# Gate and up projections of a mixture-of-experts stage as three fp32r products

## The chip, the cores and the metric

One core of a Trainium2 chip runs the whole program. The metric is device time in microseconds: the median of three runs of the kernel before is 1720.55 us (1717.99 to 1735.88). TensorE (PE in the views) does the matrix products and transposes, VectorE (DVE) and ScalarE (ACT) the elementwise work, GpSimd (POOL) and SyncE (SP) issue most of the DMAs.

## The reference

Two decoder layers over 1024 rows of width 1024. Each has a token mixer and then a mixture of experts in which every row goes to 2 of 16 experts of inner width 256:

```python
x = x + jnp.concatenate([att, pool], axis=-1) @ w_out[l]
h = rms_norm(x, norm2_gain[l])
# router: one of 4 groups, then two of its 4 experts, gates = softmax weights
hg = jnp.einsum('td,edf->tef', t, w_gate)
hu = jnp.einsum('td,edf->tef', t, w_up)
a = jax.nn.silu(hg) * hu * gates[..., None]
y = jnp.einsum('tef,efd->td', a, w_down)
x = x + y
```

The token mixer is h @ w_in (four groups of 512 columns), an attention of 8 heads over a dilated mask, and a pooling group. All is float32.

## The kernel before

Each engine runs a program of its own, written by hand; semaphores join them. One loop over the two layers holds five stages: input projection, attention, pooling and output projection with the router's logits, routing, experts.

In the input and output projections each factor is already split into a high part (a copy rounded to fp32r) and a low part (the float32 value minus it), and three fp32r products (high x high, high x low, low x high) are added in PSUM. ScalarE makes the high part of the weights (in_high, L661), VectorE the low part (in_low, L938).

**Experts.** The (row, expert) pairs are sorted into blocks of 128 rows of one expert: at most 31 (BLOCKS), of which the first `used` count. The first 16 are unconditional (`SURE`), each later one is under a comparison with `used`. In the order of each engine, for block t:
- GpSimd gathers the rows of a block from DRAM with an indirect DMA (load_rows, L608) as soon as a slot of a ring of three is free, and adds the result of a block five earlier to the output with another (add_rows, L618).
- TensorE (moe_pe, L1591): gate_up(t), one float32 product per 128 of K, so 8 of 128x512 into PSUM bank 2, 16 passes in the trace (L1566), on weights that stay where the DMA put them; xtm(t+1), eight transposes of the next block's rows (L1340); down(t-1), four products 128x512 (L1579); two transposes of the activation of t.
- ScalarE (moe_act, L841): Silu (L843); half of the y copy of t-1 (moe_down, L834), then a wait for y0_ready, y1_ready and the landed additions (s_add); then aT (L847), the transposed activation that down(t) reads.
- VectorE (moe_dve, L1281): rows_evac(t+1), the transposed rows times norm2's gain in two instructions of 128x512 (L905); the activation product (L1285); y_evac(t-1), its half of y (L1270).

The weights of an expert (gate, up and down, 1 MB each) lie in one of four slots. SyncE issues the load of expert e+4 when the down product of expert e's last block is done, and reports expert e+3 after that (report, w_loaded):

```python
sp.wait_ge(dn_done, upto(l, BLOCKS, ended))                      # L516
load_expert(e, slot)
report((slot - 1) % SLOTS, g if i else g - 1)
```

TensorE reads the expert of a block from the table block_e into a register, waits for w_loaded, and works out the address (weights, L1557). After the last block, the rest of the 31 are passed through the conditional's other branch on every engine, and the next layer's first rows are read back (L461), squared (L657) and normalised.

**Around it.** While routing runs, SyncE loads the first 512 columns of the next layer's w_in (L504), ScalarE and VectorE split them (L828, L1279). The gate of each listed row comes out of 16 small products (L1586) that stand before gate_up(0). In the attention VectorE evacuates part of the transposed probabilities (half_evac, L1057) and adds the mask and takes the maximum of the scores two row blocks ahead (mask, L1040), in that order. In the output projection it normalises each row tile (L1134) and scales its transposed columns by the gain (gain2, L1108).

## Time and profile before

| | |
|---|---|
| median of three runs | 1720.55 us |
| profiled execution, its own time | 1728.34 us |
| its span, first to last instruction | 1726.4 us |
| TensorE busy | 1493.9 us (87%) |
| VectorE, ScalarE, GpSimd busy | 782.2, 453.9, 315.3 us |
| gate and up products, L1566 (720 passes) | 325.8 us |
| down products, L1579 (360 passes) | 165.2 us |
| chain that ended last | PE 76%, DVE 8%, issue 7%, DMA 3% |
| DMA | 221.09 MB, mean 128 GB/s |

The profiled execution is one run with the hardware profiler on. Busy times are unions of an engine's records; records of TensorE overlap, so the pitch between starts, not the length of a record, is what one product costs. "Issue" is time in which an engine waited for nothing that the profile shows. The expert stage of layer 0 runs from about 558 to 826 us, that of layer 1 from about 1404 to 1684 us.

### The profile page before, as it was taken

What the parts mean: (1) busy time and instruction counts of PE and PEld (TensorE: products, weight loads), DVE (VectorE), ACT (ScalarE), POOL (GpSimd) and SP (SyncE); (2) the same over time, 40 slices, a digit from 0 to 9 for tenths busy, and PEclk for the clock granted to TensorE, in tenths of its full rate; (3) what the DMA queues carried; (4) which work ended last, traced back from release to release, by engine and by line L of the source; (5) the groups of instructions that cost most, each with busy time, mean ns of one, the idle gap of its engine ahead of it and who ended that gap; (6) DMA issues with size and microseconds to landing.
All of it is one profiled execution on the core that took longest, in us unless ns stands there. A gap on an engine that the chain in (4) does not pass through costs nothing.

```text
span 1726.4 us, 22556 instructions
## 1 busy us (share of the span) xinstructions
PE 1493.9 (87%) x6963; PEld 1080.2 (63%) x6964; DVE 782.2 (45%) x1883; ACT 453.9 (26%) x886; POOL 315.3 (18%) x204
## 2 busy tenths in 40 slices
PE   5999978998993999999389998889899759999990
PEld 4878868886882444444178786788788624444440
DVE  5777656663337122212267866666534452212210
ACT  4231245762111011111222313557412101111110
POOL 1000067001000122222500002930200012222224
PEclk9999989999995999999599999999999869999995
DMA  8000020000168599973960002000002945999947
GB/s 313 18 1 0 0 98 1 2 1 1 73 225 286 163 286 297 339 216 85 233 214 0 1 0 98 1 1 2 1 26 96 332 143 161 272 297 287 307 86 159
DMA packets 116624, 221.09 MB, mean 128 GB/s; under 512 B 5976, under 2 KB 72736, under 8 KB 116544
## 3 DMA queue, kind: packets, MB, share of 16 engines
q1 hardware_dynamic: 91744, 131.82, 22.1%
q0 software_dynamic: 19136, 69.38, 16.5%
q10 hardware_dynamic: 5664, 18.88, 2.8%
q8 instruction: 44, 0.72, 0.2%
q14 instruction: 36, 0.29, 0.1%
HBM read 170.77 MB, written 49.28 MB: 127 GB/s over the span
## 4 chain that ended last, share of the span: by engine, by line
PE 76%; DVE 8%; issue 7%; DMA 3%; ACT 2%; POOL 1%; ACTq 1%; DVEq 0%; PEld 0%; PEldq 0%; POOLq 0%; SPq 0%
PE ps L1566 19%; PE ps L1360 17%; PE ps L1340 10%; PE ps L1493 10%; PE ps L1579 9%; PE ps L1446 6%; PE ps L1420 2%; PE ps L1507 2%; DMA out_x<-x_res,arena 2%; PE ps L1422 1%; POOL out_x L622 1%; DVE k_high L1031 1%; DVE arena L1149 1%; PE ps L1480 1%; DVE w_in_lo L944 1%
## 5 line engine op out<-in xcount | busy, mean ns | idle before, releaser
L1566 PE MATMUL ps<-big,arena 128*128 x720 | 325.8, 606 | 9.7 <-issue 8.3
L1340 PE MATMUL ps<-cst,arena 128*128 128x128 f32 x1242 | 186.8, 286 | 78.2 <-DVE arena L915 36.4
L1566 PEld LDWEIGHTS ps<-big,arena 128*128 128x128 f32 x720 | 135.8, 194 | 170.5 <-issue 170.5
L905 DVE TENSOR_TENSOR arena<-ps,par 128x512 f32<-128x512 f32 x126 | 81.1, 686 | 355.6 <-PE ps L1340 355.6
L1340 PEld LDWEIGHTS ps<-cst,arena 128*128 128x128 f32 x1242 | 153.0, 147 | 125.3 <-DVE arena L915 38.1
L1360 PE MATMUL ps<-w_in_hi,hT_hi 128*128 128x512 f32 x512 | 206.1, 403 | 13.2 <-DVE hT_lo L933 10.5
L1360 PE MATMUL ps<-w_in_lo,hT_hi 128*128 128x512 f32 x512 | 202.1, 395 | 0.0
L1360 PE MATMUL ps<-w_in_hi,hT_lo 128*128 128x512 f32 x512 | 201.9, 394 | 0.0
L614 POOL DMA_INDIRECT x_res<-token_rows,row_tok x62 | 61.0, 984 | 607.0 <-issue 310.3
L1579 PE MATMUL ps<-big,arena 128*128 x360 | 165.2, 602 | 5.4 <-issue 5.4
L1446 PE MATMUL ps<-big,arena 128*128 128x64 f32 x1152 | 148.5, 276 | 0.0
L1446 PEld LDWEIGHTS ps<-big,arena 128*128 128x128 f32 x1152 | 145.2, 199 | 1.3
L622 POOL DMA_INDIRECT out_x<-x_res,arena x62 | 102.8, 1658 | 170.3 <-ACTq L839 141.1
L1052 DVE CUSTOM_DVE_ANT_0 arena<-ps,cst 128x128 f32<-128x128 f32 (+7 forms) x128 | 96.3, 752 | 56.0 <-PE ps L1422 55.5
L754 ACT ACTIVATE arena<-arena,st 128x128 f32<-128x128 f32 (+7 forms) x128 | 98.9, 772 | 82.5 <-DVE st L1052 82.0
L1360 PEld LDWEIGHTS ps<-w_in_hi,hT_hi 128*128 128x128 f32 x512 | 97.8, 191 | 35.5 <-issue 12.0
L1579 PEld LDWEIGHTS ps<-big,arena 128*128 128x128 f32 x360 | 66.0, 194 | 72.4 <-issue 72.4
L1360 PEld LDWEIGHTS ps<-w_in_hi,hT_lo 128*128 128x128 f32 x512 | 97.8, 191 | 21.2
L1493 PE MATMUL ps<-w_o_hi,cat_hi 128*128 128x512 f32 x256 | 104.1, 407 | 7.2 <-DVE cat_lo L1115 7.2
L1360 PEld LDWEIGHTS ps<-w_in_lo,hT_hi 128*128 128x128 f32 x512 | 98.0, 191 | 19.4
L1493 PE MATMUL ps<-w_o_lo,cat_hi 128*128 128x512 f32 x256 | 101.5, 396 | 0.0
L1493 PE MATMUL ps<-w_o_hi,cat_lo 128*128 128x512 f32 x256 | 101.3, 396 | 0.0
(169 smaller groups left out, 1771.3 us busy)
## 6 DMA issues: line engine op xcount, KB each, us to landing
big<-in_w_gate SPq DMA_DIRECT2D x32, 1024.0 KB, 7.9
big<-in_w_up SPq DMA_DIRECT2D x32, 1024.0 KB, 12.7
big<-in_w_down SPq DMA_DIRECT2D x32, 1024.0 KB, 15.4
big<-in_w_in SPq DMA_DIRECT2D x16, 1024.0 KB, 9.9
big<-in_w_out SPq DMA_DIRECT2D x4, 2048.0 KB, 10.2
token_rows<-arena ACTq DMA_DIRECT2D x16, 512.0 KB, 3.2
out_x<-x_res ACTq DMA_DIRECT2D x16, 512.0 KB, 3.9
x_res<-out_x SPq DMA_DIRECT2D x8, 512.0 KB, 6.0
```

What stands on the lines that cost most here:

```text
L614: pool.indirect_dma_start(out=xg[slot], out_offset=None, in_=token_rows, in_offset=bass.IndirectOffsetOnAxis(ap=row_tok[:, j:j + 1], axis= ...
L622: pool.indirect_dma_start(out=out, out_offset=bass.IndirectOffsetOnAxis(ap=row_dst[:, j:j + 1], axis=0), in_=y[j % RING], in_offset=None, ...
L754: sc.activation(pr[m % 3][:, 0:nk], pr[m % 3][:, 0:nk], ACT.Exp, scale=-1.0, bias=st[:, 64 + m % 16:65 + m % 16], accum_out=st[:, 80 + m % ...
L905: ins = ve.tensor_tensor(out=dst[:, 4 * h:4 * h + 4, :], in0=ps[:, banks + h, :].rearrange("p (a c) -> p a c", c=P), in1=spread(gain[:, 4 ...
L1052: ve.tensor_tensor_reduce(out=pr[m % 3][:, 0:nk], in0=ps[:, 2 * b:2 * b + 2, :].rearrange("p a c -> p (a c)")[:, 0:nk], in1=cst[:, C_MASK ...
L1340: ins = te.transpose(ps[:, bank + i // 4, (i % 4) * P:(i % 4 + 1) * P], src, ident)
L1360: ins = te.matmul(ps[:, 2 + 2 * par_ + i, :], a[par_][:, k, :], b[:, k, :], start=k == 0 and n == 0, stop=k == K - 1 and n == 2)
L1420: te.matmul(ps[:, 2 * b + c // 512, 0:w], q_parts[a][:, i * P:(i + 1) * P], k_high[a][:, c:c + w], start=True, stop=False)
L1446: ins = te.matmul(ps[:, 6 + hd % 2, i * HD:(i + 1) * HD], prT[b][:, j, :], v[:, j, hd * HD:(hd + 1) * HD], start=j == 0, stop=j == i)
L1493: ins = te.matmul(ps[:, 2 * par_ + h, :], a[par_][:, k, :], b[:, k, :], start=k == 0 and n == 0, stop=k == K - 1 and n == 2)
L1566: ins = te.matmul(ps[:, 2, :], xgT[:, k, :], big[:, ds(at + k * 2 * FE, 2 * FE)], start=k == 0, stop=k == K - 1)
L1579: ins = te.matmul(ps[:, 4 + h, :], aT[:, k, :], big[:, ds(at + (E_GU + k * D + 512 * h), 512)], start=k == 0, stop=k == 1)
```

## The change

The gate and up product becomes 24 fp32r products of 128x512. The weights of a block are split in halves of 128x2048 (K 0 to 3 and 4 to 7): gu_high on ScalarE, gu_low on VectorE, into a ring of three halves, high and low each. They are split again for every block, also where it has the same expert as the one before. A half is overwritten when the product of the half three before is done (gu_half). The rows are split too: rows_high on ScalarE, rows_evac on VectorE, one instruction of 128x1024 each, into xgT_hi and xgT_lo. Both gu_high and gu_low read the block's expert from block_e into a register each time. The gain of norm2 is multiplied into the rows before they are stored (gain2_row, a broadcast load), not after the transposes. The first input weights of the next layer are loaded when expert 12 has ended, and split after the last block. list_gates moves behind gate_up(0), and mask before half_evac.

```diff
-        xgT = A[:, 3072:4096].rearrange("p (k n) -> p k n", n=P)
-        sg, act = A[:, 4096:4352], A[:, 4352:4608]
+        xgT_hi = nc.alloc_sbuf_tensor_at("xgT_hi", [P, D], f32r, offset=xr_start)[:, :].rearrange("p (k n) -> p k n", n=P)
+        xgT_lo = nc.alloc_sbuf_tensor_at("xgT_lo", [P, D], f32r, offset=xr_start + 4 * D)[:, :].rearrange("p (k n) -> p k n", n=P)
+        HALF_GU = K * 2 * FE // 2
+        gu_hi = [part(f"gu_hi{i}", at, HALF_GU) for i, at in enumerate((0, 2 * HALF_GU, AT_A))]
+        gu_lo = [part(f"gu_lo{i}", at + HALF_GU, HALF_GU) for i, at in enumerate((0, 2 * HALF_GU, AT_A))]
+        gain2_row = A[:, 0:D]
+        experts = big[:, :]
+        sg, act = A[:, 7904:8160], A[:, 4352:4608]
...
@@ -475,6 +488,7 @@
                 sp.wait_ge(rows_t, 1)
                 sp.wait_ge(x_ready, upto(l, T, T))
                 load_in(l, 2, 1)
+                sp.wait_ge(win_split, upto(l, 8, 2))
...
+                sp.dma_start(gain2_row, norm2_gain[ds(l, 1), :].to_broadcast([P, D])).then_inc(s_gain2, 16)
...
-                load_in((l + 1) % DEPTH, 0, 0)
...
                 report(1, NE // SLOTS - 1)
+                with sp.If(l < DEPTH - 1):
+                    ended = sp.value_load(start_i[0:1, NE - 3:NE - 2], min_val=0, max_val=BLOCKS)
+                    sp.wait_ge(dn_done, upto(l, BLOCKS, ended))
+                    load_in((l + 1) % DEPTH, 0, 0)
...
-                in_high(l + 1, 0)
...
+                def gu_high(t, slot, h):
+                    e = a_.value_load(block_e[0:1, ds(t, 1)], min_val=0, max_val=NE - 1)
+                    a_.wait_ge(w_loaded, upto(l, NE, e + 1))
+                    a_.sem_inc(s_passed, 1)
+                    at = ((e + 2) % SLOTS) * E_ALL + AT_E
+                    sc.activation(gu_hi[(2 * slot + h) % 3], experts[:, ds(at + h * HALF_GU, HALF_GU)],
+                                  ACT.Copy).then_inc(gu_top, 1)
+                def rows_high(t):
+                    a_.wait_ge(xtm_done, upto(l, BLOCKS, t + 1))
+                    sc.activation(xgT_hi, ps[:, 0:2, :].rearrange("p a (k n) -> p (a k) n", n=P), ACT.Copy)\
+                        .then_inc(xg_top, 1)
...
                 def moe_act(t, slot, m):
+                    if not last(t, BLOCKS):
+                        gu_high(t + 1, (slot + 1) % RING, 0)
+                        a_.wait_ge(gu_half, upto(l, BLOCKS, t + 1))
+                        a_.sem_inc(s_passed, 1)
+                        gu_high(t + 1, (slot + 1) % RING, 1)
                     a_.wait_ge(gu_done, upto(l, BLOCKS, t + 1))
                     sc.activation(sg, ps[:, 2, 0:FE], ACT.Silu).then_inc(silu_done, 1)
+                    if not last(t, BLOCKS):
+                        a_.wait_ge(xgT_ready, upto(l, BLOCKS, t + 1))
+                        rows_high(t + 1)
                     if not first(t):
                         moe_down(t - 1, *before(slot, m))
...
+                for h in range(2):
+                    gu_high(0, 0, h)
+                for i in range(2):
+                    a_.wait_ge(s_tok[i], (l + 1) * (16 * (T // 2)) + 1)
+                    a_.sem_inc(s_passed, 1)
+                a_.wait_ge(s_base, (l + 1) * (16 * T))
+                a_.sem_inc(s_passed, 1)
+                rows_high(0)
...
                     ch.restart()
+                    in_high(l + 1, 0)
...
@@ -1077,10 +1131,10 @@
                 mask(1)
                 for m in range(ROWS_A):
                     p, n = m // 16, m % 16
+                    if m + 2 < ROWS_A:
+                        mask(m + 2)
                     if m % T >= 4:
                         half_evac(m)
-                    if m + 2 < ROWS_A:
-                        mask(m + 2)
                     if m >= T and m % T == 1:
...
-                    times_gain(h2T[par_], par[:, G2:G2 + K], 4, h2T_ready)
+                    ve.tensor_copy(h2T[par_], ps[:, 4:6, :].rearrange("p a (k n) -> p (a k) n", n=P)).then_inc(h2T_ready, 1)
...
-                    ve.tensor_scalar(xs2[par_], xr[:, t, :], r, None, ALU.mult).then_inc(xs2_ready, 1)
+                    ve.scalar_tensor_tensor(out=xs2[par_], in0=xr[:, t, :], scalar=r, in1=gain2_row,
+                                            op0=ALU.mult, op1=ALU.mult).then_inc(xs2_ready, 1)
...
+                def gu_low(t, slot, h):
+                    dve.wait_ge(gu_top, upto(l, 2 * BLOCKS, 2 * t + h + 1))
+                    dve.sem_inc(s_passed, 1)
+                    e = dve.value_load(block_e[0:1, ds(t, 1)], min_val=0, max_val=NE - 1)
+                    at = ((e + 2) % SLOTS) * E_ALL + AT_E
+                    i = (2 * slot + h) % 3
+                    ve.tensor_tensor(out=gu_lo[i], in0=experts[:, ds(at + h * HALF_GU, HALF_GU)],
+                                     in1=gu_hi[i].bitcast(f32), op=ALU.subtract).then_inc(gu_split, 1)
+                for h in range(2):
+                    gu_low(0, 0, h)
...
                 def rows_evac(t):
-                    dve.wait_ge(xtm_done, upto(l, BLOCKS, t + 1))
-                    times_gain(xgT, par[:, G2:G2 + K], 0, xgT_ready)
+                    dve.wait_ge(xg_top, upto(l, BLOCKS, t + 1))
+                    ve.tensor_tensor(out=xgT_lo, in0=ps[:, 0:2, :].rearrange("p a (k n) -> p (a k) n", n=P),
+                                     in1=xgT_hi.bitcast(f32), op=ALU.subtract).then_inc(xgT_ready, 1)
...
-                in_low(l + 1, 0)
                 def moe_dve(t, slot, m):
                     if not last(t, BLOCKS):
-                        rows_evac(t + 1)
+                        for h in range(2):
+                            gu_low(t + 1, (slot + 1) % RING, h)
                     dve.wait_ge(silu_done, upto(l, BLOCKS, t + 1))
                     ve.scalar_tensor_tensor(out=act, in0=ps[:, 2, FE:2 * FE], scalar=list_gate[:, ds(t, 1)], in1=sg,
                                             op0=ALU.mult, op1=ALU.mult).then_inc(a_ready, 1)
+                    if not last(t, BLOCKS):
+                        rows_evac(t + 1)
                     if not first(t):
                         y_evac(t - 1, *before(slot, m))
...
                 with dve.If(l < DEPTH - 1):
+                    in_low(l + 1, 0)
...
-                def gate_up(t):
-                    at = weights(t)
+                def gate_up(t, slot):
                     for k in range(K):
-                        ins = te.matmul(ps[:, 2, :], xgT[:, k, :], big[:, ds(at + k * 2 * FE, 2 * FE)],
-                                        start=k == 0, stop=k == K - 1)
+                        h = k // (K // 2)
+                        if k % (K // 2) == 0:
+                            pe.wait_ge(gu_split, upto(l, 2 * BLOCKS, 2 * t + h + 1))
+                        c = slice(k % (K // 2) * 2 * FE, (k % (K // 2) + 1) * 2 * FE)
+                        hi, lo = gu_hi[(2 * slot + h) % 3][:, c], gu_lo[(2 * slot + h) % 3][:, c]
+                        for n, (a, b) in enumerate(((xgT_hi, hi), (xgT_hi, lo), (xgT_lo, hi))):
+                            ins = te.matmul(ps[:, 2, :], a[:, k, :], b, start=k == 0 and n == 0,
+                                            stop=k == K - 1 and n == 2)
+                        if k == K // 2 - 1:
+                            ins.then_inc(gu_half, 1)
                     ins.then_inc(gu_done, 1)
...
                 xtm(0, 0, 0)
-                pe.wait_ge(gate_parts, upto(l, 1, 1))
-                for c in range(2 * T):
-                    ins = te.matmul(ps[:, 7, 0:96], in_row[:, c, :], in_gate[:, c, :, :].rearrange("p k b -> p (k b)"),
-                                    start=c == 0, stop=c == 2 * T - 1)
-                ins.then_inc(gates_listed, 1)
                 used = pe.value_load(start_i[0:1, NE:NE + 1], min_val=2 * SEQ // P, max_val=BLOCKS)
+                def list_gates():
+                    pe.wait_ge(gate_parts, upto(l, 1, 1))
+                    for c in range(2 * T):
+                        ins = te.matmul(ps[:, 7, 0:96], in_row[:, c, :],
+                                        in_gate[:, c, :, :].rearrange("p k b -> p (k b)"),
+                                        start=c == 0, stop=c == 2 * T - 1)
+                    ins.then_inc(gates_listed, 1)
                 def moe_pe(t, slot, m):
                     pe.wait_ge(xgT_ready, upto(l, BLOCKS, t + 1))
                     if not first(t):
                         pe.wait_ge(a_ready, upto(l, BLOCKS, t))
                     pe.sem_inc(s_passed, 1)
-                    gate_up(t)
+                    gate_up(t, slot)
+                    if first(t):
+                        list_gates()
```

Line numbers in the order listings below are those of each version; L1339 of after is y_evac, L886 is aT, L865 the half of y on ScalarE, L859 rows_high, L1333 rows_evac, L1354 the activation product.

ScalarE, body of the loop over blocks, before:

```order
L843 ACTIVATE arena<-ps 128x256
L832 ISA
L833 ISA
L834 ACTIVATE x_res<-ps 128x512
L838 ISA
L847 ACTIVATE arena<-ps 128x256
```

and after, up to the register read of the next turn:

```order
L854 ACTIVATE gu_hi_75<-big 128x2048
L879 ACTIVATE arena<-ps 128x256
L858 ISA
L859 ACTIVATE xgT_hi<-ps 128x1024
L863 ISA
L864 ISA
L865 ACTIVATE x_res<-ps 128x512
L869 ISA
L886 ACTIVATE arena<-ps 128x256
L850 ISA
L850 TENSOR_LOAD block_e
L850 ISA x2
```

The copy of aT (L847, now L886) is followed by a register read (TENSOR_LOAD) and the first high half of the block after the next, where only the next wait for TensorE stood.

VectorE, body of the same loop, before:

```order
L1264 ISA
L905 TENSOR_TENSOR arena<-ps,par 128x512 x2
L1285 ISA
L1285 SCALAR_TENSOR_TENSOR arena<-ps,arena 128x256
L1269 ISA
L1270 COPY x_res<-ps 128x512
```

and after, from the register read of the second half on:

```order
L1303 TENSOR_LOAD block_e
L1303 ISA x2
L1306 ISA
L1306 TENSOR_TENSOR gu_lo_78<-big,gu_hi_75 128x2048
L1353 ISA
L1354 ISA
L1354 SCALAR_TENSOR_TENSOR arena<-ps,arena 128x256
L1332 ISA
L1333 TENSOR_TENSOR xgT_lo<-ps,xgT_hi 128x1024
L1337 ISA
L1338 ISA
L1339 COPY x_res<-ps 128x512
```

The rows' evacuation moved behind the activation product, and two subtractions with a register read each stand before it.

VectorE at the start of the expert stage, before (block_e is the table of experts, gate_w the gates whose bits are taken apart):

```order
L1238 TENSOR_SCALAR block_e<-arena 128x32
L1243 ISA
L1246 TENSOR_SCALAR arena<-gate_w 128x16
L1247 TENSOR_SCALAR arena<-gate_w 128x16
L1248 TENSOR_SCALAR arena<-gate_w 128x16
L1249 CAST arena<-arena 128x48
```

and after:

```order
L1294 TENSOR_SCALAR block_e<-arena 128x32
L1301 ISA
L1303 TENSOR_LOAD block_e
L1303 ISA x2
L1306 ISA
L1306 TENSOR_TENSOR gu_lo_76<-big,gu_hi_73 128x2048
L1301 REGISTER_ALU
L1303 TENSOR_LOAD block_e
L1303 ISA x2
L1306 ISA
L1306 TENSOR_TENSOR gu_lo_77<-big,gu_hi_74 128x2048
L1311 ISA
```

Both subtractions of block 0 now stand between the table of experts and the gate bits.

## Rows read from the trace of the kernel before

**Rows 1.** The chain of waits, one block: start us, us, what
```profile
619.40 6.87 PE ps L1566 x16
...
627.14 3.44 PE ps L1579 x8
630.58 0.22 PE ps L1340 x2
```

**Rows 2.** Windows: length, busy us per engine (instructions), clock, DMA share
```profile
280.00:390.00 110.00, 104.06 (x807) 96.66 (x806) 68.05 (x145) 74.08 (x156) 14.71 (x5) 0.99 0.01 1
570.00:820.00 250.00, 244.08 (x716) 117.61 (x714) 49.79 (x84) 29.02 (x64) 53.00 (x42) 0.99 0.80 239
640.00:650.00 10.00, 9.93 (x31) 4.73 (x30) 0.94 (x2) 1.36 (x3) 2.00 (x2) 1.00 1.06 358
```

**Rows 3.** TensorE timeline, input projection: start us, us, engine line operation
```profile
108.66 0.39 PE L1360 MATMUL ps<-w_in_hi,hT_lo 128*128 128x512 f32 x1
108.88 0.39 PE L1360 MATMUL ps<-w_in_hi,hT_hi 128*128 128x512 f32 x1
```

**Rows 4.** Timeline, the operations that price a split of weights and rows
```profile
532.82 3.69 ACT L667 ACTIVATE w_in_hi<-big 128x2048 fp32r<-128x2048 f32 x2
...
514.87 1.22 DVE L1127 TENSOR_TENSOR x_res<-ps,x_res 128x1024 f32<-128x1024 f32 x1 [4.17 <-PE ps L1493]
...
558.15 4.49 DVE L944 TENSOR_TENSOR w_in_lo<-big,w_in_hi 128x2048 fp32r<-128x2048 f32 x2
```

**Rows 5.** Timeline of ScalarE and VectorE in the expert stage, one block
```profile
650.30 1.29 DVE L905 TENSOR_TENSOR arena<-ps,par 128x512 f32<-128x512 f32 x2 [7.60 <-PE ps L1340]
651.51 0.47 DVE L1285 SCALAR_TENSOR_TENSOR arena<-ps,arena 128x256 f32<-128x256 f32 x1
653.89 0.69 DVE L1270 COPY x_res<-ps 128x512 f32<-128x512 f32 x1 [1.91 <-PE ps L1579]
...
654.83 0.39 ACT L847 ACTIVATE arena<-ps 128x256 f32<-128x256 f32 x1 [0.37 <-DVE x_res L1270]
```

**Rows 6.** First product; register reads, ns min/median/max, first and last start
```profile
558.53 8.58 PE L1566 MATMUL ps<-big,arena 128*128 x16 [1.25 <-issue]
...
L1559 PEldq TENSOR_LOAD <-block_e x5: 298/303/310, 641.3 to 663.8; - x5
...
L1260 DVEq TENSOR_LOAD <-start_i x2: 326/438/550, 554.4 to 1399.7; - x2
```

**Rows 7.** Timeline, start of the expert stage: routing known, gate bits, second product
```profile
549.96 0.18 DVE L1238 TENSOR_SCALAR block_e<-arena 128x32 int32<-128x32 f32 x1
...
554.12 0.19 DVE L1258 SCALAR_TENSOR_TENSOR arena<-ps,arena 128x32 int32<-128x32 f32 x1
...
571.45 8.83 PE L1566 MATMUL ps<-big,arena 128*128 x16 [1.25 <-issue]
```

**Rows 8.** Timeline of SyncE's queue: two loads of expert weights, first and last transfer
```profile
1568.88 0.37 SPq L486 DMA_DIRECT2D big<-in_w_gate  x1
...
1570.08 1.95 SPq L489 DMA_DIRECT2D big<-in_w_down  x1
...
1603.68 0.37 SPq L486 DMA_DIRECT2D big<-in_w_gate  x1
...
1606.37 5.46 SPq L489 DMA_DIRECT2D big<-in_w_down  x1
```

**Rows 9.** Timeline of ScalarE at the end of layer 0
```profile
846.45 1.28 ACT L877 ACT_TABLE_LOAD   x1 [20.12 <-ACTq L857]
```

**Rows 10.** Timeline of VectorE in the attention
```profile
353.92 0.56 DVE L1062 COPY arena<-ps 128x384 f32<-128x384 f32 x1 [1.32 <-PE ps L1340]
```

**Rows 11.** Timeline of GpSimd and VectorE, start of layer 1
```profile
854.94 1.55 POOL L622 DMA_INDIRECT out_x<-x_res,arena  x1 [0.30 <-issue]
856.80 5.89 POOL L622 DMA_INDIRECT out_x<-x_res,arena  x1 [0.31 <-issue]
...
856.78 4.48 DVE L944 TENSOR_TENSOR w_in_lo<-big,w_in_hi 128x2048 fp32r<-128x2048 f32 x2
```

24 lines of the change are left out of this document (20 added, 4 removed).

## The prediction

> **What bounds the kernel now.** I read the page first: TensorE is busy 87% of the span and holds 76% of the chain that ended last, so the chain, followed through the expert stage, comes next. There every block of 128 rows is the same four pieces on TensorE with nothing between them: 16 passes of the gate and up product in 6.87 us, eight transposes in the 0.87 up to 627.14, the down product 3.44, two transposes 0.22 [rows 1]. That is 11.40 us a block, and the windows show TensorE busy 244 of 250 us there, with VectorE at 20% and ScalarE at 12% [rows 2]. The count of the passes (720 = 45 x 16) gives 45 blocks, 22 in layer 0 and 23 in layer 1. The DMA engines are the second resource: while every block has an expert of its own they stand at a share of 1.06 and 358 GB/s [rows 2]. So TensorE is the bound, the transfers are close behind it, and ScalarE and VectorE have some 9 us a block to spare. That spare time is what the change spends.
>
> **The product itself.** A 128x512 fp32r product is recorded at 0.39 us, but the records overlap: in the input projection they start every 0.227 us [rows 3]. Gate and up become 24 of them: 24 x 0.227 = 5.45 us in place of 6.87. If TensorE stayed the bound a block would take 5.45 + 0.87 + 3.44 + 0.22 = 9.98 us, 1.42 less, or 64 us over 45 blocks. That is the ceiling, not the forecast.
>
> **The loop that the change closes.** Each block's weights must now be split: two 128x2048 copies on ScalarE (3.69 for two, 1.85 each) and two 128x2048 subtractions on VectorE (4.49 for two, 2.24 each) [rows 4]. Look at the order around them. On VectorE a turn of the loop is: first subtraction, second subtraction, the activation product, the rows' low part, and only then the copy of y from PSUM. On ScalarE the copy of aT waits for that y copy (its wait for y0_ready), and the next block's first high half stands behind aT; VectorE's next first subtraction waits for that half. So the loop runs through both engines and holds one block:
> - activation product to rows' low part, 0.40 (a 0.47 record, 0.08 overlapped, as all pitches on VectorE);
> - rows' low part, 128x1024 with one input in PSUM. Nearest row: 1.22 for the same shape in the output projection [rows 4]; pitch 1.14. Floor: the two 128x512 evacuations, of which the second ends 1.29 after the start and the next starts at 1.21 [rows 5];
> - y copy 0.69, and from its end to the start of aT 0.25 (653.89 + 0.69 to 654.83) [rows 5];
> - aT's start to the first high half: a register read of the block's expert lies between. On TensorE the same read with its wait and addresses leaves 1.25 us idle when nothing covers it [rows 6]; on ScalarE 0.38 of it runs under aT's own 0.38. I take 1.0;
> - the high half, 1.85;
> - its end to the first subtraction: a register read on VectorE, bare. The read proper is 0.14 longer there than on TensorE (0.44 and 0.30), and no register has to be waited for [rows 6]; I take 1.1;
> - first subtraction 2.24, second 2.20. The second one's register read is taken as hidden under the first, because TensorE reads block_e while its own matmuls still run (five reads in a stretch without a gap, 0.30 each) [rows 6].
>
> Sum: 0.40 + 1.14 + 0.69 + 0.25 + 1.0 + 1.85 + 1.1 + 2.24 + 2.20 = 10.87 us. That is longer than TensorE's 9.98, so TensorE idles 0.9 us a block and the block costs 10.87, only 0.53 less than now. Bounds: register reads that cost 0.3 each give 9.5, and then TensorE's 9.98 holds; a second read that is not hidden gives 11.9. With 41 blocks behind the first two of each layer: -0.53 x 41 = **-22 us**, bounds -58 and +20.
>
> **The start of each expert stage.** The first two splits stand on VectorE before the gate bits. Routing is known at 550.14 [rows 7]. Two register reads on ScalarE, 0.9 each, put the first high half at 552.0 to 553.9, VectorE's two subtractions at 555.0 to 559.5, the gate bits (3.8 us, now ending at 554.31 [rows 7]) behind them to 563.3, a register read to 564.2, the rows' low part to 565.4. The product starts at 565.5 where it started at 558.53 [rows 6]: 7 us late. Then the list of gates, moved behind it on TensorE, and the second block's subtractions, which stand behind its evacuation, hold the first activation product: 565.5 + 7.5 (at part clock, as the 8.58 and 8.83 us of the first two blocks now) + 0.75 + 0.8 + 0.9 + 4.5 + 1.6 = 581.8, against 571.45 [rows 7]. The second block's shorter product returns about 1. **+9.4 us** a layer, 19 in all; bounds 6 and 13 a layer.
>
> **Expert loads.** Four slots hold weights, and load e+4 is issued when expert e ends. The report that expert e+3 is in comes only after that load is queued. Queueing takes 3.1 us on a quiet queue (1568.88 to 1572.03) and 8.2 behind an unfinished load (1603.68 to 1611.83) [rows 8]. Now the report is wanted at the start of block b+3, b being e's last block, when the two experts between have one block each; after the change ScalarE wants it a block earlier, at its high half, some 3.0 us after the down product that frees the slot. Ten first blocks stand so (five in each layer, by the issue times); these two are the shortest and the longest queueing among them, which is 0.1 to 5.2 too much, some 22 us in all. A wait lets the transfers catch up, so neighbours do not add; a shorter block makes them lag more (a load with a block's rows takes some 12.1 us at 358 GB/s: 4.2 MB). I take 7 a layer, **+14 us**, bounds 4 and 30.
>
> **The rest.** At the layer's end ScalarE comes to its table load at 846.45 straight from its own queue [rows 9], and TensorE waits for what follows. The split of the first input weights, which lay in the routing stage, now stands before it: two copies, 3.7 us, **+4**, once. In the attention the mask two row blocks ahead no longer stands behind the evacuation of the second half, which waits for transposes (1.32 us in [rows 10]). TensorE idles 5.9 of 110 us there [rows 2], so at most 7 a layer come back; I take **-3** for both, bounds 0 and -10. Folding norm2's gain makes the normalised rows a two-tensor operation (about 1.2 for 0.75), on the path for the last tile alone: **+1**. The 2 MB load and its split that leave the routing stage cost nothing now: VectorE did that split (558.15 to 562.64) under the first product [rows 4]. The broadcast of the gain (0.5 MB) has a projection of 11 us to land under.
>
> Sum: -22 + 19 + 14 + 4 - 3 + 1 = +13 us on the profiled execution's 1728.3 us, which is 0.5% above the median of 1720.55: **1734 us** as a median.
>
> **A rule against the change.** The two indirect DMAs of each block are generated on GpSimd, an addition in 1.55 us. One took 5.89: it started at 856.80, with two VectorE subtractions of SBUF tensors from 856.78 to 861.26 [rows 11]. After the change every block has such a pair. The Trainium skill (SBUF — State Buffer, Who interferes with whom) says that a VectorE operation with two SBUF inputs takes only the read side from GpSimd, and infers that descriptor generation goes on beside it. By that rule the sum stays; by the row each block's gather or addition can come 4.3 us late. The measurement decides. A gather has two blocks of slack, and an addition starts at 1.7 us of a block, ahead of the subtractions at 4.9, so my sum holds no term for it.
>
> **The rivals.**
> - *Register reads are cheap (0.30).* For: one VectorE read took only 0.33, and queues can run ahead. Against: 1.25 us stood bare on TensorE [rows 6]. The loop is then 9.5 to 10.3 and TensorE holds near 10.1: -1.3 x 41 = -53, but the waits for loads grow (+22): -53 + 19 + 22 + 2 for the rest = -10, 1711 us; with the start and the attention at their kind bounds (-6, -7), 1698.
> - *VectorE's second read is bare (0.18), the other side.* For: every read in VectorE's rows stands behind a wait, none under a running operation. A read that waits for the engine to drain adds 1.0 to the loop: 11.9 us. It decides from 11.4 us a block: above that the blocks lose. +0.5 x 41 = +20, hardly a wait for loads (+1): 20 + 19 + 1 + 2 = +42, 1762 us.
> - *Transfers or additions are the bound (0.15).* Runs of one-block experts go at 12.1 us, each with a queueing wait, or the additions of [rows 11] come late: 12 us more than forecast, some 1748. For: shares of 1.06. Against: pauses of several blocks in the loads.
> - *Forecast (0.37)*: 1722 to 1748.
>
> **How the numbers follow.** About 1% is what a measurement here can tell from no change: 1703 to 1738. Faster by over 1%: somewhat over half of the first rival (1698 to 1722, with its middle at 1711; the loop's terms leave more room below than above), 0.18. Slower by over 1%: nearly all of the second rival (0.16), most of the third (0.11) and three tenths of the forecast's case (0.11): 0.38. Within: 0.44. Range: from the cheap reads with the kind start, 1700, to the bare read, 1762.
>
> **What would show it.** Product starts 0.227 apart at 24 a block; a block of 10.9 us with 0.9 idle on TensorE, released by VectorE's low part; VectorE near 80% busy; the first product near 565; high halves that wait for a load where two one-block experts precede; PE restart at the layer's end 4 us later against the last down product. Blocks of 10.1 or 11.9 would break the loop's terms, and a start within 3 us of now the second term.

## The result, and the profile after

The changed kernel's median is 1784.05 us (four runs, 1772.11 to 1789.20) against 1728.22 for the kernel before in the same session: a recorded ratio of 1.028, 95% interval 1.023 to 1.034 (the two medians alone give 1.032). It is slower, by more than the 1% that can be told, and above the predicted range (1700 to 1762). In all ratios, runs more than 1.5% above the fastest run of the same kernel are left out. Its profiled execution took 1789.2 us, span 1787.3: 61 us more than the span before, and the longest of its four runs. Parts that vary from run to run are therefore also read from the experiments below.

From the page of the changed kernel, busy times, chain, and groups (line, engine, operation, count, busy us, mean ns, idle before and its releaser):

```profile
PE 1454.7 (81%) x7323; PEld 1154.7 (65%) x7324; DVE 987.4 (55%) x1913; ACT 669.6 (37%) x1026; POOL 363.6 (20%) x204
...
PE 53%; DVE 14%; issue 12%; ACT 8%; DVEq 3%; DMA 3%; ACTq 3%; SPq 2%; POOL 1%; PEld 0%; PEldq 0%; POOLq 0%
...
L1306 DVE TENSOR_TENSOR gu_lo<-big,gu_hi 128x2048 fp32r<-128x2048 f32 x94 | 212.9, 2291 | 255.6 <-issue 227.8
...
L854 ACT ACTIVATE gu_hi<-big 128x2048 fp32r x94 | 179.2, 1915 | 152.4 <-issue 127.3
L632 POOL DMA_INDIRECT x_res<-token_rows,row_tok x62 | 111.3, 1795 | 598.6 <-issue 310.2
...
L1644 PE MATMUL ps<-gu_hi,xgT_hi 128*128 128x512 f32 x360 | 153.0, 425 | 61.3 <-DVE xgT_lo L1333 61.3
```

TensorE is busy 39 us less, and holds 53% of the chain instead of 76%. VectorE, ScalarE, their queues and "issue" hold 40%. Before the subtractions stand 255.6 idle us, 227.8 of them ended by the engine's own issue. The window of the expert stage, one of those of [rows 2], in the changed kernel (span, us, busy time and count of TensorE, its weight loads, VectorE, ScalarE and GpSimd, granted clock, DMA share, GB/s):

```profile
570.00:820.00 250.00, 213.80 (x867) 146.28 (x866) 133.96 (x103) 124.44 (x122) 73.05 (x39) 0.96 0.81 242
```

TensorE, 244 of 250 us busy before, is now busy 214. Its granted clock in this window is 0.96 where it was 0.99. One unstalled block of layer 0, timeline of VectorE and ScalarE (start, length, both in us, idle before in brackets):

```profile
604.05 0.48 DVE L1354 SCALAR_TENSOR_TENSOR arena<-ps,arena 128x256 f32<-128x256 f32 x1
...
605.57 0.68 DVE L1339 COPY x_res<-ps 128x512 f32<-128x512 f32 x1
...
606.48 0.38 ACT L886 ACTIVATE arena<-ps 128x256 f32<-128x256 f32 x1 [0.79 <-DVE x_res L1339]
...
607.50 1.92 ACT L854 ACTIVATE gu_hi<-big 128x2048 fp32r x1 [0.64 <-issue]
...
610.07 1.92 ACT L854 ACTIVATE gu_hi<-big 128x2048 fp32r x1 [0.65 <-issue]
...
610.57 4.68 DVE L1306 TENSOR_TENSOR gu_lo<-big,gu_hi 128x2048 fp32r<-128x2048 f32 x2 [4.31 <-issue]
...
615.16 0.48 DVE L1354 SCALAR_TENSOR_TENSOR arena<-ps,arena 128x256 f32<-128x256 f32 x1
```

Activation products at 604.05 and 615.16: the block takes 11.11 us, where it took 11.40. The next one, at whose start the hardware loop turns (every third block):

```profile
619.28 3.94 ACT L854 ACTIVATE gu_hi<-big 128x2048 fp32r x2 [1.01 <-issue]
...
623.29 4.49 DVE L1306 TENSOR_TENSOR gu_lo<-big,gu_hi 128x2048 fp32r<-128x2048 f32 x2 [5.92 <-ACT gu_hi L854]
...
627.70 0.48 DVE L1354 SCALAR_TENSOR_TENSOR arena<-ps,arena 128x256 f32<-128x256 f32 x1
```

12.54 us. The first high half ends at 621.21 and the first subtraction starts at 623.29, 2.1 us later, where 1.1 lay in the block before (609.42 to 610.57). The chain of waits names the piece, a register read of VectorE, and below it stands what the same line takes in all (min, median and max in ns):

```profile
619.28 1.93 ACT gu_hi L854
...
621.53 1.23 DVEq L1303
```

```profile
L1303 DVEq TENSOR_LOAD <-block_e x94: 298/311/1409, 552.2 to 1730.5; - x94
```

19 of VectorE's reads in this run took over 0.5 us (most of them 1.0 to 1.4), 15.8 us more together than at the median. Each is the first of its block's two reads, the one that stands behind the wait for the first high half. Ten are in conditional blocks, four in blocks at the loop's turn, one is the stage's first, and four are in other blocks. The stage's start, [rows 5 to 7] of before:

```profile
552.16 1.97 PE L1413 MATMUL ps<-cst,x_res 128*128 128x128 f32 x8 [6.02 <-DMA x_res<-token_rows,row_tok]
553.32 4.49 DVE L1306 TENSOR_TENSOR gu_lo<-big,gu_hi 128x2048 fp32r<-128x2048 f32 x2 [5.00 <-issue]
...
562.25 1.23 DVE L1333 TENSOR_TENSOR xgT_lo<-ps,xgT_hi 128x1024 fp32r<-128x1024 f32 x1 [0.76 <-DVE arena L1326]
...
563.75 0.79 PE L1644 MATMUL ps<-gu_hi,xgT_hi 128*128 128x512 f32 x1 [9.62 <-DVE xgT_lo L1333]
...
572.04 0.85 PE L1669 MATMUL ps<-arena 128*128 128x96 f16 x16
...
574.67 4.54 DVE L1306 TENSOR_TENSOR gu_lo<-big,gu_hi 128x2048 fp32r<-128x2048 f32 x2 [1.03 <-issue]
...
579.14 0.47 DVE L1354 SCALAR_TENSOR_TENSOR arena<-ps,arena 128x256 f32<-128x256 f32 x1
...
581.24 0.79 PE L1644 MATMUL ps<-gu_hi,xgT_hi 128*128 128x512 f32 x1 [0.88 <-DVE xgT_lo L1333]
```

From the transposes of the first rows to activation product 0 it is 27.0 us (before 554.03 to 569.23, 15.2). And the layer's end, issues of SyncE among it:

```profile
840.16 6.60 PE L1659 MATMUL ps<-big,arena 128*128 x8 [3.31 <-issue]
...
854.93 0.94 SPq L450 DMA_DIRECT2D big<-in_w_in  x2
...
856.83 3.41 SPq L474 DMA_DIRECT2D x_res<-out_x  x2
...
863.79 3.71 ACT L685 ACTIVATE w_in_hi<-big 128x2048 fp32r<-128x2048 f32 x2 [16.20 <-ACTq L899]
...
884.60 1.06 ACT L675 ACTIVATE arena<-x_res 128x1024 f32<-128x1024 f32 x1 [15.59 <-SPq L477]
...
888.13 1.97 PE L1413 MATMUL ps<-cst,arena 128*128 128x128 f32 x8 [41.37 <-DVE arena L969]
```

Stage lengths, from activation product to activation product, and the boundary from the last one to TensorE's restart (us, from the traces):

| kernel | layer 0, 21 blocks | boundary | layer 1, 22 blocks |
|---|---|---|---|
| before | 245.8 | 36.4 | 258.0 |
| changed | 256.7 | 52.3 | 272.2 |
| changed, loads cut by a third (e4) | 248.1 | 51.7 | 261.1 |
| reads ahead (e3) | 235.7 | 48.8 | 250.4 |
| one read on ScalarE (e10) | 248.3 | 48.7 | 270.9 |
| reads ahead on VectorE (e11) | 236.8 | 52.9 | 247.4 |
| three edits (e8) | 235.6 | 38.1 | 247.3 |
| three edits, loads cut (e9) | 226.8 | 37.9 | 243.5 |
| three edits, gate and up loads early (e12) | 223.9 | 38.0 | 235.9 |

Three other runs whose stage code is the changed kernel's (e1, e5, e7) have 250.2, 252.3, 251.1 in layer 0 and 272.1, 269.3, 272.6 in layer 1.

### The profile page after: what moved, and what is told of

The parts are those of the page before. It is cut to its first block, busy times and chain, and to the rows that moved or that the text cites. A ratio compares the mean times of both kernels' runs of the same rounds, so it can differ in the third digit from the quotient of the medians.

```text
span 1787.3 us, 24347 instructions
## 1 busy us (share of the span) xinstructions
PE 1454.7 (81%) x7323; PEld 1154.7 (65%) x7324; DVE 987.4 (55%) x1913; ACT 669.6 (37%) x1026; POOL 363.6 (20%) x204
## 4 chain that ended last, share of the span: by engine, by line
PE 53%; DVE 14%; issue 12%; ACT 8%; DVEq 3%; DMA 3%; ACTq 3%; SPq 2%; POOL 1%; PEld 0%; PEldq 0%; POOLq 0%
PE ps L1433 17%; PE ps L1566 9%; PE ps L1413 8%; PE ps L1644 6%; PE ps L1519 6%; ACT gu_hi L854 5%; DVE gu_lo L1306 2%; DVE xgT_lo L1333 2%; PE ps L1493 2%; DVEq L1303 2%; DMA x_res<-out_x 2%; ACTq L850 1%; PE ps L1495 1%; PE ps L1580 1%; SPq L503 1%
## 5 line engine op out<-in xcount | busy, mean ns | idle before, releaser
L1306 DVE TENSOR_TENSOR gu_lo<-big,gu_hi 128x2048 fp32r<-128x2048 f32 x94 | 212.9, 2291 | 255.6 <-issue 227.8
L1413 PE MATMUL ps<-cst,arena 128*128 128x128 f32 x1242 | 189.6, 287 | 127.1 <-DVE arena L969 52.3
L854 ACT ACTIVATE gu_hi<-big 128x2048 fp32r x94 | 179.2, 1915 | 152.4 <-issue 127.3
L632 POOL DMA_INDIRECT x_res<-token_rows,row_tok x62 | 111.3, 1795 | 598.6 <-issue 310.2
L1644 PE MATMUL ps<-gu_hi,xgT_hi 128*128 128x512 f32 x360 | 153.0, 425 | 61.3 <-DVE xgT_lo L1333 61.3
L1659 PE MATMUL ps<-big,arena 128*128 x360 | 168.0, 611 | 6.6 <-issue 6.6
L1519 PEld LDWEIGHTS ps<-big,arena 128*128 128x128 f32 x1152 | 146.8, 201 | 1.2
L1644 PE MATMUL ps<-gu_lo,xgT_hi 128*128 128x512 f32 x360 | 147.2, 409 | 0.0
L1644 PE MATMUL ps<-gu_hi,xgT_lo 128*128 128x512 f32 x360 | 147.1, 409 | 0.0
L640 POOL DMA_INDIRECT out_x<-x_res,arena x62 | 98.9, 1594 | 173.0 <-ACTq L870 149.2
L1644 PEld LDWEIGHTS ps<-gu_hi,xgT_hi 128*128 128x128 f32 x360 | 72.3, 201 | 87.0 <-issue 72.7
L1433 PEld LDWEIGHTS ps<-w_in_hi,hT_hi 128*128 128x128 f32 x512 | 97.8, 191 | 35.0 <-issue 11.7
L1659 PEld LDWEIGHTS ps<-big,arena 128*128 128x128 f32 x360 | 67.1, 196 | 74.9 <-issue 74.9
```

Of the source, the lines that this page charges most:

```text
L632: pool.indirect_dma_start(out=xg[slot], out_offset=None, in_=token_rows, in_offset=bass.IndirectOffsetOnAxis(ap=row_tok[:, j:j + 1], axis= ...
L640: pool.indirect_dma_start(out=out, out_offset=bass.IndirectOffsetOnAxis(ap=row_dst[:, j:j + 1], axis=0), in_=y[j % RING], in_offset=None, ...
L854: sc.activation(gu_hi[(2 * slot + h) % 3], experts[:, ds(at + h * HALF_GU, HALF_GU)], ACT.Copy).then_inc(gu_top, 1)
L1306: ve.tensor_tensor(out=gu_lo[i], in0=experts[:, ds(at + h * HALF_GU, HALF_GU)], in1=gu_hi[i].bitcast(f32), op=ALU.subtract).then_inc(gu_sp ...
L1413: ins = te.transpose(ps[:, bank + i // 4, (i % 4) * P:(i % 4 + 1) * P], src, ident)
L1433: ins = te.matmul(ps[:, 2 + 2 * par_ + i, :], a[par_][:, k, :], b[:, k, :], start=k == 0 and n == 0, stop=k == K - 1 and n == 2)
```

## The experiments

Each ratio is against the kernel before, run beside it. The intervals of e1, e4, e5, e7 and e10 overlap that of the changed kernel (1.023 to 1.034): for these the times alone don't tell the two kernels apart, and the reading rests on the traces and on the kernels that join several edits.

**Which register reads.** Three kernels. In gu_high, one read for both halves; in gu_low, one read ahead of the wait for the first high half:

```diff
 # ScalarE (e10, e3)
+                        e = a_.value_load(block_e[0:1, ds(t + 1, 1)], min_val=0, max_val=NE - 1)
-                        gu_high(t + 1, (slot + 1) % RING, 0)
+                        gu_high(t + 1, (slot + 1) % RING, 0, e)
...
 # VectorE (e11, e3)
+                        e = dve.value_load(block_e[0:1, ds(t + 1, 1)], min_val=0, max_val=NE - 1)
                         for h in range(2):
-                            gu_low(t + 1, (slot + 1) % RING, h)
+                            gu_low(t + 1, (slot + 1) % RING, h, e)
```

> The changed kernel, with one register read of the block's expert on ScalarE (used for both high halves) instead of two, and one on VectorE ahead of the wait for the first high half instead of two behind the waits. Theory (the loop through ScalarE and VectorE runs over both high halves with every read bare): the loop of 11.1 us loses 0.65 us on ScalarE and 0.5 to 0.7 us on VectorE, so blocks come at the matrix unit's own 9.98 to 10.1 us where nothing else is late, and the time falls by 20 to 45 us to some 1740 to 1765. Rival 1 (expert loads set the pace: 12.1 us from one expert's landing to the next): blocks with an expert of their own stay at about 12 us and the gain is under 15 us. Rival 2 (the reads cost nothing, the pace is set by something else in the loop): no change.

Measured: ratio 1.002 [0.998, 1.007], from 1.028: some 45 us, the upper end of what was expected, and both rivals fell. Then the two apart:

> The changed kernel with one register read a block on ScalarE instead of two; VectorE's two reads stay behind their waits. It tells which engine's reads the 44 us of both belong to. Theory (the loop runs through both high halves and then the second subtraction, with 0.65 us of bare read between the halves on ScalarE and 1.1 us between the first half's end and the first subtraction on VectorE): ScalarE's read alone gives 0.65 us in most of 43 blocks, -20 to -28 us, about 1760. Rival (the loop runs through VectorE's first read and its two subtractions back to back, as in the prediction's loop, and the second high half is hidden beside the first subtraction): under 5 us.

Measured: ratio 1.029 [1.023, 1.035], no change.

> The changed kernel with one register read a block on VectorE ahead of the wait for the first high half, and ScalarE's two reads as they were. Theory (the last subtraction starts when the second high half is done and its own read is over): VectorE's reads give what is left of the 44 us, -16 to -24 us, about 1764. Rival (the reads on VectorE alone carry the loop): -35 us or more, about 1745; rival (ScalarE's alone do): under 5 us.

Measured: ratio 1.005 [1.001, 1.009], some 40 us less. The theory, that both engines share the loss, fell: VectorE's reads carry nearly all. The blocks show why. With ScalarE's read alone gone (e10):

```profile
601.20 0.48 DVE L1355 SCALAR_TENSOR_TENSOR arena<-ps,arena 128x256 f32<-128x256 f32 x1
...
604.68 3.72 ACT L853 ACTIVATE gu_hi<-big 128x2048 fp32r x2 [0.65 <-issue]
...
607.71 4.49 DVE L1307 TENSOR_TENSOR gu_lo<-big,gu_hi 128x2048 fp32r<-128x2048 f32 x2 [4.30 <-issue]
...
612.12 0.48 DVE L1355 SCALAR_TENSOR_TENSOR arena<-ps,arena 128x256 f32<-128x256 f32 x1
```

The two high halves go back to back, but the first subtraction still starts 1.1 us after the first of them, and 4.49 us for the pair sets the activation product: 10.92 us. In the changed kernel the second high half was only 0.2 us off being hidden (4.68 us for the pair of subtractions there, 4.49 here). With VectorE's reads ahead (e11), at the loop's turn:

```profile
615.16 0.48 DVE L1355 SCALAR_TENSOR_TENSOR arena<-ps,arena 128x256 f32<-128x256 f32 x1
...
619.28 3.96 ACT L854 ACTIVATE gu_hi<-big 128x2048 fp32r x2 [1.00 <-issue]
...
621.54 4.49 DVE L1305 TENSOR_TENSOR gu_lo<-big,gu_hi 128x2048 fp32r<-128x2048 f32 x2 [4.17 <-ACT gu_hi L854]
...
625.95 0.48 DVE L1355 SCALAR_TENSOR_TENSOR arena<-ps,arena 128x256 f32<-128x256 f32 x1
```

```profile
L1351 DVEq TENSOR_LOAD <-block_e x45: 301/307/324, 575.0 to 1680.2; - x45
```

ScalarE's copies start at the same distance as in the changed kernel, and the subtraction follows at 621.54 instead of 623.29. This block takes 10.79 us instead of 12.54, plain ones 10.4 instead of 11.1, and the conditional ones at the end of layer 0's stage 10.5 to 11.1 instead of 11.3 to 12.4. Moved ahead of the wait, no read of the loop is longer than 0.33 us. So the reads' price is 0.7 us in a plain block and 1 to 1.8 where the long reads were. In e10 the long reads stayed, 18 of them.

**Loads.** Half of the gate and up weights of experts 4 to 15 are not loaded:

```diff
-                        load_expert(e, slot)
+                        load_expert(e, slot, K // 2)
```

> The changed kernel, leaving out half of the gate and up weights of experts 4 to 15 in each layer (their loads move 2 MB instead of 3 MB; the products of those halves use what an earlier expert left). Theory (loop as it stands, with loads late only at some blocks): the two stalls of 17 us and the 12.4 to 12.8 us blocks after them go, steady blocks stay at 11.1 us, and the two expert stages lose 20 to 25 us together: about 1760. Rival (loads set the pace nearly everywhere): the stages lose 40 us or more. Rival (loads never decide): under 5 us.

Measured: ratio 1.021 [1.013, 1.029]. ScalarE's waits for load reports (us in total, times, longest), layer 0, of the changed kernel and of this one:

```profile
ACT gu_hi L854 <- SPq L510: 12.5, 4, 6.9
```

```profile
ACT gu_hi L854 <- SPq L510: 2.8, 4, 0.9
```

The changed kernel's two longest blocks, 17.1 and 17.0 us, each with a wait of 6.9 or 6.8 us for a report, are gone, and the stages are 8.6 and 11.1 us shorter than in the profile of the changed kernel, 2 to 4 and 8 to 12 shorter than in e1, e5 and e7. So the third of the loads that is left out costs 10 to 20 us, less than the 20 to 25 expected except against the profile of the changed kernel. Not all waits are gone: 4.7 us for load reports remain in the two stages. The same cut on the kernel before:

> The kernel before, leaving out half of the gate and up weights of experts 4 to 15 in each layer (2 MB instead of 3 MB an expert). Theory (before the change no block waited for a load, and transfers beside the products cost them nothing): within 3 us of the kernel before, and the same 11.4 us pitch. Rival (the traffic slows the row transfers or the products even there): 5 us or more.

Measured: ratio 1.006 [1.001, 1.010], with 11.40 us a block as before and stages of 244.0 and 258.0 (the 1.8 us less in layer 0 lie in its first block, 11.47 for 13.16). So no block before the change lost time to a load. The time is not within the expected 3 us: it is some 10 us above the kernel before by the ratio. In its trace the extra time lies in the attention (last section), not in the stages.

**The layer's end.** First the row reload was put ahead of the weight load:

```diff
                         sp.dma_start(xr[:, t, :], out[t * P:(t + 1) * P, :]).then_inc(s_again[t], 16)
...
+                    sp.wait_ge(dn_done, upto(l, BLOCKS, used - BLOCKS))
+                    sp.wait_ge(gu_split, upto(l, 2 * BLOCKS, 0))
+                    load_in(l, 1, 2)
                     for t in range(2):
```

> The changed kernel, with the second layer's first 2 MB weight load (third quarter of w_in) issued after the reload of the first two row tiles instead of ahead of it. Theory (the new wait for the last weight split holds that load until 854.9 us and puts it in front of the row reload, whose landing the first square of layer 2 then waits for, 15.59 us at 884.60): the restart of TensorE at the layer's end comes 14 to 18 us earlier than 41.4 us of idle time, and the time falls from 1784 to about 1768. Rival (the load of the first quarter and the additions of expert rows fill the queues anyway): the reload lands as late as before and the time stays within 3 us of 1784.

Measured: ratio 1.026 [1.017, 1.034]. TensorE's idle time fell from 41.37 to 25.65 us, as expected, but part came back: the second half of w_in's quarter is now late,

```profile
865.55 1.89 ACT L684 ACTIVATE w_in_hi<-big 128x2048 fp32r<-128x2048 f32 x1
...
875.12 1.91 ACT L684 ACTIVATE w_in_hi<-big 128x2048 fp32r<-128x2048 f32 x1 [7.67 <-DMA big<-in_w_in]
```

and from restart to layer 1's activation product 0 it is 580.4 us, 7.2 more than in the changed kernel. The span fell by 14.5 us, of which 6.5 lie in layer 0's stage, that the edit doesn't touch. So the new wait itself was taken out. It is not needed: the last block's down product comes after all subtractions of its layer.

```diff
                     sp.wait_ge(dn_done, upto(l, BLOCKS, used - BLOCKS))
-                    sp.wait_ge(gu_split, upto(l, 2 * BLOCKS, 0))
                     load_in(l, 1, 2)
```

> The changed kernel without the wait for the last weight split ahead of the second layer's 2 MB load of the third quarter of w_in, so that this load is issued when the last block's down product is done, as in the kernel before. Theory (that one wait is what makes the layer's end longer): the load is issued 8 us after the last down product begins instead of after the passed blocks, the row reload finds the queues clear, TensorE restarts about 36.5 us after the last activation product instead of 52.3, and unlike with the reload moved forward nothing comes later in layer 2's first products: -16 us, about 1768. Rival (what the layer's end lost is the transfer of the first quarter, 2 MB, which the changed kernel issues only after the last expert): the restart stays beyond 45 us and the time falls by under 8 us.

Measured: ratio 1.024 [1.018, 1.030].

```profile
837.81 6.50 PE L1658 MATMUL ps<-big,arena 128*128 x8 [3.31 <-issue]
...
844.52 0.94 SPq L450 DMA_DIRECT2D big<-in_w_in  x2
...
865.09 3.71 ACT L684 ACTIVATE w_in_hi<-big 128x2048 fp32r<-128x2048 f32 x2 [19.95 <-DMA out_x<-x_res,arena]
...
873.74 1.97 PE L1412 MATMUL ps<-cst,arena 128*128 128x128 f32 x8 [29.42 <-DVE arena L968]
```

The load goes out right after the down product, and the boundary is 40.2 us instead of 52.3: 12.1 of the 16 us expected. The 3.8 left over 36.4 fit the split of the first input weights (3.71 on ScalarE), but they are not its price in every kernel: e8, e9 and e12 have the same split and boundaries of 37.9 to 38.1.

**The start.** Gate bits ahead of block 0's subtractions, and the list of gates ahead of block 0's product:

```diff
-                for h in range(2):
-                    gu_low(0, 0, h)
                 dve.wait_ge(s_base, (l + 1) * (16 * T))
...
                 ins.then_inc(gate_parts, 1)
+                for h in range(2):
+                    gu_low(0, 0, h)
...
                     gate_up(t, slot)
-                    if first(t):
-                        list_gates()
```

> The changed kernel with its start of the expert stage alone put back in the old order: the gate bits on VectorE ahead of block 0's two subtractions, and the product that lists the gates ahead of block 0's gate and up products. Theory (the 10 us that each stage starts late are VectorE's order: 4.5 us of gate bits behind 4.5 us of subtractions while it had been idle for 5.0 us before them, then a wait for the listed gates that holds block 1's first subtraction until 574.67): first product near 559.5 instead of 563.75, activation product 0 near 569.5 instead of 579.14, so -9 us a layer, -18 us in all, about 1766. Rival (weight splits of ScalarE and the half clock set the start): first product at 559.5 to 562, activation product 0 not before 575, -4 us a layer.

Measured: ratio 1.025 [1.019, 1.031]; first product at 559.48, activation product 0 at 570.06, 19.0 us after the first transposes instead of 27.0; in layer 1 19.9 instead of 25.5. The theory holds, at 13.6 us for both layers, not 18.

**Attention's mask alone**, on the kernel before (mask ahead of half_evac):

> The kernel before, with only the order of the mask and the half evacuation in attention changed. The prediction's term: -3 us in all, bounds 0 to -10, so a time of about 1725 where the kernel before has 1728. The trace of the changed kernel shows the first layer's attention ending some 3 us earlier; if that is the mask's doing in both layers, -6 us; if it came from something else, 0.

Measured: ratio 0.993 [0.990, 0.996], 7 to 17 us; its profiled span is 3.0 us shorter. The times give the sign, but the trace doesn't show the cause: from the first product of the input projection to the first of the output projection it has 391.8 us in layer 0 against 389.2 in the kernel before, and 393.6 against 394.9 in layer 1, and 2.3 of the 3.0 us lie after the last activation product of layer 1.

**Together.** Reads ahead (e3), no wait for the split (e5), the old order at the start (e7):

> The changed kernel with three edits together: reads of the block's expert ahead (one on each engine), no wait for the last split ahead of the second layer's weight load, and the old order at the stage's start. Theory (the three losses lie behind one another in time and add): 1784 - 44 - 16 - 18 = 1706 us, some 1.3% below the kernel before. Rival (the loads of expert weights take the start's gain back, since they are not issued earlier): the stage ends when the last experts' loads allow and the start's 18 us shrink to 5, about 1720.

Measured: 1711.98 us, where 1706 was expected, ratio 0.990 [0.986, 0.993]: 1% faster than the kernel before.

> The same three edits, leaving out half of the gate and up weights of experts 4 to 15 in each layer (2 MB instead of 3 MB an expert; those halves' products use an earlier expert's weights). Theory (with the loop under TensorE's pace, what is left over 10.1 us a block is loads, 12.1 us from one expert's landing to the next where experts have one block): both stages come down to 22 and 23 blocks of 10.1 to 10.6 us, 25 to 30 us under the run with full loads. Rival (the third block of each turn and the conditional blocks cost it, not the loads): under 8 us.

Measured: ratio 0.979 [0.973, 0.986], stages 8.8 and 3.8 us shorter. Loads still cost something, between the two expectations. Then the gate and up slots were refilled earlier, which the ring of split halves allows, as the raw weights aren't read after the split:

```diff
+                        sp.wait_ge(gu_done, upto(l, BLOCKS, ended))
+                        load_gate_up(e, slot)
                         sp.wait_ge(dn_done, upto(l, BLOCKS, ended))
-                        load_expert(e, slot)
+                        load_down(e, slot)
```

> The kernel with the three edits, and its gate and up loads issued when the gate and up product of the last block of that slot's former expert is done, instead of its down product one block later; the down weights' load keeps its wait. Theory (13 to 18 us of the two stages are waits for loads that are issued too late to be back in time for a split one block ahead): a head start of some 12 us at each load takes most of it back: -8 to -15 us, about 1700. Rival (the transfers' rate, 12.1 us for 3 MB beside the row transfers, is the bound where experts have one block each, so an earlier issue only lengthens the queue): under 4 us.

Measured: 1684.26 us, ratio 0.973 [0.968, 0.978]. Windows and waits:

```profile
570.00:790.00 220.00, 211.78 (x873) 146.37 (x874) 135.80 (x101) 125.81 (x123) 70.23 (x40) 1.00 0.91 276
```

```profile
ACT gu_hi L861 <- SPq L516: 1.3, 2, 0.6
```

TensorE is busy 96% of this window at full clock with 24 fp32r products a block, and most blocks come at 10.2 to 10.8 us (some at 11 to 12.3). It beats the expectation: e12's stages are 11.7 and 11.4 us shorter than e8's, also shorter than with a third of the loads left out. In both stages together ScalarE waits 32.5 us for load reports in e8 (10 times) and 4.1 in this one (5 times). The transfers' rate was not the bound; the time of issue was.

## Why the prediction was wrong

It said +13 us on the profiled execution and a median of 1734; measured were +61 and 1784. The sign was right, and so were the product's pace, a plain block, the start and the loads; one term was mis-sized and one step missed.

- **The product.** Starts lie 0.227 us apart (641.08, 641.30, 641.53 in the changed kernel), 5.45 us for 24. As predicted, and TensorE's 9.98 us a block is nearly reached where nothing is late (10.13 in e3 and e8).
- **The loop: the step that failed.** "With 41 blocks behind the first two of each layer: -0.53 x 41 = -22 us." The loop of a plain block was right: 10.92 us in e10 for 10.87 predicted, with the first read on VectorE bare at 1.1 and the second hidden; ScalarE's second read, which the sum left out, makes it 11.1. But that is a plain block, and it was multiplied by all. With loads cut (e4) layer 0's stage has blocks of 11.1 us, 11.3 to 12.6 where a read is long or the loop turns, and 11.8 to 13.4 in the six conditional ones; the kernel before has 11.4, 11.75 and 11.8 to 12.3. The stages then last 2.3 and 3.1 us longer than before: the term is **+5 at most, not -22**, mis-sized by some 27 us. Of that, up to 17 us are the long reads on VectorE (23 in e4's trace, 17.6 us over the median, one of them ahead of the loop), which the sum priced like the plain ones. ScalarE's second read, 0.2 in a plain block, would be 8 us over 41 blocks (an estimate), and 4.7 us are the waits for loads that e4 still has. Reading VectorE's register ahead of the wait brings some 40 us (e11). Why reads behind that wait are long in some blocks was not found; in the same blocks, ahead of it, they are not.
- **The start.** +9.4 a layer predicted; against the first transposes, activation product 0 is 11.8 and 9.7 us late. Right, and by the cause named: e7 takes two thirds of it back. That product 1 starts at 581.24 for 581.8 predicted is partly luck: the first transposes start 1.9 us earlier than before, and the prediction's own terms add to 581.55. What the sum did not have is the clock: TensorE was granted 0.52 from 560 to 570 us and 0.67 from 580 to 590, where it had 0.93 and 1.00 before and 0.87 and 1.00 in e7 (0.5 is the lower of its two levels, 1.2 GHz). It had stood 9.62 us before the first product.
- **Loads.** +14 predicted, bounds 4 and 30; 10 to 20 measured for the third that e4 leaves out. (4.2 MB at 358 GB/s are 11.7 us, not the 12.1 in the prediction; the term doesn't hang on it.)
- **The layer's end: the step that was missed.** +4 was predicted for the split of the first input weights; 3.8 are left in e5 and 1.5 to 1.7 in e8, e9 and e12. The new wait for gu_split ahead of load_in(l, 1, 2) was not costed. For the layer just ended it asks for the last of all 31 blocks' counts, so SyncE stands until VectorE has passed the empty blocks (854.93), and its 2 MB go out 1.9 us ahead of the row reload, whose landing then holds ScalarE for 15.59 us. In the kernel before the load was out at 825.68 and the reload at 839.63. **+12 us.**
- **Attention.** -3 predicted. From the input projection to the output projection, layer 0 takes 386.3 us in the profile against 389.2 before, but layer 1 395.2 against 394.9, and the other traces with the mask moved have 386.3 to 391.8 in layer 0, e2 the longest. So no trace shows this term; the times of e2 give at least 7 us, and their cause is open.
- **The rule against the change.** The Trainium skill (SBUF — State Buffer, Who interferes with whom) would have descriptor generation go on beside a VectorE operation with two SBUF inputs. The gathers of rows don't go on undisturbed: 984 ns in the mean before, they take 1795 ns. The 45 that overlap a subtraction of gu_lo take 2.06 us in the mean, up to 3.08; of the 17 that overlap none, 16 take 0.94 to 1.10. Whether the descriptors or the reading of the row indices stands still, the trace doesn't tell. It cost TensorE nothing, as the prediction said: its only waits for a gather, 12 us in two, are at the start of the two stages, as before. For the additions the row stays untested, since none overlaps a subtraction of gu_lo.
- **A sign that misled.** "VectorE near 80% busy": it is busy 54% of the window, and the prediction's own terms give 62% (6.7 of 10.87 us). The longer read on VectorE (0.44) came from two reads of another table; its reads of block_e take 0.31 in the median, though the bare 1.1 us up to the subtraction held.

Added up as the profile has them: 21.5 (start) + 19.7 (loads) + 5.4 (loop) + 15.9 (end) - 1.9 (ahead of layer 0's first transposes) = 60.6 of its 61 us. The profile was a long run of its kernel, the loads above all: against e1, e5 and e7 they are 12 to 15 us. By the ratio, 2.8% of 1728, the kernel's loss is 49 us. Of the rivals, "VectorE's second read is bare" came nearest in time (+42) but not in mechanism: e10 shows the second read hidden.

## What to carry to other kernels

When a change closes a loop through two engines, work out the loop for each kind of iteration, the turn and the conditional ones too, and multiply by their own counts: what an engine hides in its queue, a closed loop pays each time. Read registers ahead of the wait that the read doesn't depend on. Cost every new wait on the queue that issues transfers by when it can be met at its latest, and by which transfers then go out together; and when a copy frees its source early, refill the source then.

## What the runs showed of the hardware

VectorE's reads of an entry of block_e took 0.30 to 1.41 us behind a wait in the loop and 0.30 to 0.32 ahead of it, as shown above.

A 64x1024 cast on VectorE takes 1.42 us in one run and 9.20 in another, when it falls beside a two-input subtraction of 128x4096 on GpSimd. The timeline of attention in e4b (the kernel before with cut loads, its attention unchanged), and then in the kernel before:

```profile
278.18 9.66 POOL L590 TENSOR_TENSOR w_o_lo<-big,w_o_hi 128x4096 fp32r<-128x4096 f32 x1
279.19 9.20 DVE L1031 CAST k_high<-big 64x1024 fp32r<-64x1024 f32 x1
```

```profile
270.36 1.42 DVE L1031 CAST k_high<-big 64x1024 fp32r<-64x1024 f32 x1
...
279.55 8.93 POOL L590 TENSOR_TENSOR w_o_lo<-big,w_o_hi 128x4096 fp32r<-128x4096 f32 x1
```

In the second the cast is over before GpSimd's long subtraction starts. In the first it starts 1.0 us after it and ends at 288.39, 0.55 us after the subtraction's end at 287.84: it stood until GpSimd was done. The Trainium skill (SBUF — State Buffer, Who interferes with whom) says so of a cast in a two-port mode, that the one that issues second is blocked for the other's whole instruction; the trace agrees. TensorE then waits up to 13.0 us for an evacuation behind the cast, and its granted clock is 0.79 and 0.53 in the two stretches of 10 us from 275. From the input projection to the output projection layer 0 takes 405.8 us in that run against 389.2, which is more than the 11 us by which its span is longer. The kernel before spreads from 1718 to 1756 us over all sessions, the one with the masks moved (e2) from 1717 to 1728 in twelve runs. That this meeting makes the spread, and that the mask's order avoids it, was not tested, and the record speaks partly against it: of the 14 traces only this one has a cast of k_high over 2.8 us, and e3, with the masks moved too, spreads over 23 us in ten runs.
